# A transformer stack on one core: split operands in four output and two down projections, modulation weights in wide pieces on GpSimd's queue, DeltaNet keys first

## What is computed

```python
def sqrelu_mlp(h, w1, w2):  # 1024 -> 4096 -> 1024, relu squared (mlp0 on 768 columns, mlp1 on 512)
...
h_lat = modulate(rms_norm(x_lat, norm_g[i, 0]), m_lat[:, 0], m_lat[:, 1])
y_ctx, y_lat = mla_mixer(...) or gla_mixer(...)      # end with "@ w_o": mla_out, gla_out
x_lat = x_lat + m_lat[:, 2] * rms_norm(y_lat, norm_g[i, 1])
...
# second block, layer i: mixer 0 is a gated DeltaNet, mixer 1 retention
mod = (e @ ada_w[i] + ada_b[i])[:, None, :]          # 6144 values of modulation
y = mixers[i % N_MIXERS_2](x * (1.0 + sc1) + sh1)    # end with "@ w_out": gdn_out, ret_out
x = layer_norm(DN_ALPHA * x + (1.0 + g1) * y, ln_g[i, 0], ln_b[i, 0])
y = conv_ffn(x * (1.0 + sc2) + sh2, ...)             # up 1024 -> 2 x 2816, down 2816 -> 1024
x = layer_norm(DN_ALPHA * x + (1.0 + g2) * y, ln_g[i, 1], ln_b[i, 1])
```

## Time and profile before

| what | value |
|---|---|
| median of 3 runs | 4176.59 us (4167.09 to 4179.34) |
| profiled run, its own time | 4172.41 us |
| its span, first to last instruction | 4170.6 us |
| TensorE, VectorE, ScalarE busy | 92%, 45%, 27% |
| mean granted TensorE clock | 0.966 |
| mlp0, mlp1 (stretches read) | 692.0 to 1248.2, 1773.4 to 2151.8 |
| DeltaNet pairs | 2213 to 2705 |
| ffn0 up, ffn0 down | 2793.6 to 3028.5, 3028.5 to 3206.4 |
| ffn1 up, ffn1 down | 3746.8 to 3981.7, 3983.7 to 4135.1 |

### The profile page before, as it was taken

One profiled execution on the slowest core, in us unless ns is written; L12 is line 12 of the kernel. 1 busy time (PEld: TensorE's weight loads), 2 busy tenths in 40 slices (PEclk: granted clock), 3 DMA queues, 4 the chain that ended last, 5 costly groups with the idle time before them and its releaser, 6 DMA issues.

```text
span 4170.6 us, 45563 instructions
## 1 busy us (share of the span) xinstructions
PE 3852.7 (92%) x16674; PEld 2768.1 (66%) x16674; DVE 1869.7 (45%) x3568; ACT 1113.7 (27%) x1357; POOL 0.2 (0%) x4
## 2 busy tenths in 40 slices
PE   6899997999998898799989999799998999899998
PEld 3477766999994656377765556548844778548853
DVE  1244426666664333366655445434477443124401
ACT  2111105132224222333333332334301322124301
POOL 0000000000000000000000000000000000000000
PEclk9999999999998999899999999899999999999999
DMA  4121111333330111145531111012376222213231
GB/s 152 41 72 61 66 56 56 102 111 99 101 96 31 31 35 45 44 143 150 152 117 38 41 40 31 28 51 92 104 197 173 66 79 72 71 41 101 92 91 49
DMA packets 414370, 335.19 MB, mean 80 GB/s; under 512 B 11697, under 2 KB 393009, under 8 KB 414129
## 3 DMA queue, kind: packets, MB, share of 16 engines
q1 hardware_dynamic: 408768, 326.21, 25.6%
q10 hardware_dynamic: 5489, 7.47, 0.5%
HBM read 331.55 MB, written 2.10 MB: 80 GB/s over the span
## 4 chain that ended last, share of the span: by engine, by line
PE 83%; DVE 6%; ACT 4%; issue 3%; DMA 2%; ACTq 1%; DVEq 0%; SPq 0%
PE acc L603 62%; PE sc L603 4%; DVE tab L1699 2%; PE sc L1050 2%; PE sc L634 2%; PE acc L798 1%; PE sc L772 1%; PE sc L774 1%; PE sc L637 1%; PE acc L1050 1%; PE acc L1204 1%; DMA wring<-in_mlp_w 1%; DMA tab<-in_ada_w 1%; PE sc L644 1%; ACTq L1308 1%
## 5 line engine op out<-in xcount | busy, mean ns | idle before, releaser
L603 PE MATMUL acc<-arena,wring 128*128 128x512 f32 (+2 forms) x1728 | 707.0, 571 | 39.8 <-DMA wring<-in_ffn_down 9.6
L603 PE MATMUL acc<-x_lo,w_hi 128*128 128x512 f32 (+1 forms) x1728 | 651.8, 377 | 0.0
L603 PEld LDWEIGHTS acc<-arena,wring 128*128 128x128 f32 (+1 forms) x1728 | 320.8, 190 | 386.9 <-issue 307.3
L1358 ACT ACTIVATE w_hi<-wring 128x1024 fp32r<-128x1024 f32 x264 | 264.9, 1051 | 1056.5 <-DMA wring<-in_mlp_w 484.4
L603 PE MATMUL acc<-x_hi_seq,w_hi 128*128 128x512 f32 x1216 | 485.2, 399 | 30.4 <-DVE x_lo L1822 29.8
L1816 DVE TENSOR_TENSOR w_lo<-wring,w_hi 128x1024 fp32r<-128x1024 f32 x264 | 311.5, 1222 | 386.7 <-ACT w_hi L1358 385.5
L603 PE MATMUL acc<-x_hi_seq,w_lo 128*128 128x512 f32 x1216 | 478.4, 393 | 0.0
L603 PEld LDWEIGHTS acc<-x_lo,w_hi 128*128 128x128 f32 x1728 | 329.9, 191 | 47.2 <-issue 1.3
L1699 DVE SCALAR_TENSOR_TENSOR tab<-tab,cs 128x128 f32<-128x128 f32 x960 | 316.4, 351 | 25.8 <-DVE tab L1699 0.2
L603 PEld LDWEIGHTS acc<-x_hi_seq,w_hi 128*128 128x128 f32 x1216 | 231.6, 190 | 92.5 <-issue 31.3
L603 PE MATMUL acc<-hid_hi,w_hi 128*128 128x384 f32 (+1 forms) x768 | 275.1, 358 | 0.0
(11 more groups left out here) (347 smaller groups left out, 4808.8 us busy)
## 6 DMA issues: line engine op xcount, KB each, us to landing
wring<-in_mlp_w SPq DMA_DIRECT2D x64, 1024.0 KB, 5.4
tab<-in_ada_w SPq DMA_DIRECT2D x216, 256.0 KB, 4.8
wring<-in_ffn_up SPq DMA_DIRECT2D x44, 1024.0 KB, 5.0
wring<-in_ada_w SPq DMA_DIRECT2D x12, 2048.0 KB, 7.8
wring<-in_ret_w_in SPq DMA_DIRECT2D x24, 1024.0 KB, 5.2
wring<-in_ffn_down SPq DMA_DIRECT2D x16, 1408.0 KB, 7.1
rstd<-in_ada_w SPq DMA_DIRECT2D x72, 256.0 KB, 5.3
wring<-in_gdn_w_in SPq DMA_DIRECT2D x16, 1024.0 KB, 5.7
```

The costliest lines, as they stand in the source:

```text
L603: ins = pe.matmul(o, lhsT, rhs, start=start, stop=stop)
L1358: f(w_hi[s][:, c], wring[s][:, c], ACT.Copy).then_inc(w_high, 1)
```

## The change

Four edits.

1. The four output projections and both ffn downs become stages of `SPLIT`. Output projections load groups of two units (one in ret_out), ffn downs two groups of 11 blocks a unit, with halves of 704 columns. ScalarE and VectorE make high and low parts of the mixers' outputs (`out_highs`, `out_lows`), and, pair by pair within the ffn up, of the hidden values. The parts lie over memory that is free then (`overlay`); the ups' high inputs lie in two parts of 256 columns (`x_hole`). In mla_out and gla_out the sums of squares of unit j-3 stand ahead of unit j.
2. Modulation pieces are one input block by 512 columns (256 KB, rows of 2 KB), 24 a quarter in three slots, issued by GpSimd on its own queue. Sums come three times a quarter, of 4 column blocks each.
3. ffn0_down's VectorE program puts pieces and weight splits in the order of `DOWN_PIECES`.
4. In `gdn_pair` keys are convolved, squared and normed ahead of queries, both sums of squares (units 1, 2) stand ahead of the row spreads (3, 4), and gate columns 1 (unit 8) behind the products (6, 7).

```diff
-SPLIT = ("mlp0", "mlp1", "ffn0_up", "ret_head", "ffn1_up")
+SPLIT = ("mla_out", "mlp0", "gla_out", "mlp1", "gdn_out", "ffn0_up", "ffn0_down", "ret_head", "ret_out",
+         "ffn1_up", "ffn1_down")
+HALF_COLS = {s: 1024 for s in SPLIT}
+HALF_COLS["ffn0_down"] = HALF_COLS["ffn1_down"] = HIDB * P // 4
...
+MOD_SLOTS = 3
+MOD_N = 512
+MOD_SUM_AFTER = {6: 0, 10: 1, 14: 2}
+DOWN_SUM_AFTER = {(0, 15): 0, (1, 15): 1}
+DOWN_PIECES = ((range(0, 8), range(8, 10), range(10, 14)), (range(14, 22), range(22, 24), range(0)))
...
+        @block.gpsimd
+        def _(pool):
+            for phase, ready in enumerate((16, 32, 40)):
...
+                pool.wait_ge(n_mul, ready)
+                with pool.Fori(0, 4) as it:
+                    for p in range(MOD_PIECES):
+                        i, k = divmod(p, DB)
+                        pool.wait_ge(mod_used[p % MOD_SLOTS], piece(phase, it, p))
+                        pool.dma_start(mod_w[p % MOD_SLOTS], w[:, k, bass.ds(it * (MOD_IT * MOD_N) + i * MOD_N, MOD_N)]
+                                       ).then_inc(mod_loaded[p % MOD_SLOTS], 16)
...
+            def out_proj(stage, nk, per, squares=None):
+                for j in range(8):
+                    if squares and j > 2:
+                        square_sum(*squares, [j - 3])
+                    if j % per == 0:
+                        w = split_group(stage, 0, j // per, nk, per * P)
+                    claim(pe, stage, 0, j)
+                    for k in range(nk):
+                        if j == 0:
+                            pe.wait_ge(o_split, OUT0[stage] + k + 1)
+                        if j % per == 0 and k == nk // 2:
+                            second_half(stage, 0, j // per)
+                        last = split_product(unit(stage, j), w, (j % per) * P, k, out_parts(stage, k), k == 0, k == nk - 1)
+                    last.then_inc(acc_ready, 1)
...
-                for r, (x, y) in enumerate(((d_q, d_Y), (d_k, d_U))):
+                act.wait_ge(d_conv, it * 3 + 2)
+                for j in (1, 0):
+                    act.wait_ge(qk_ready, it * 2 + j + 1)
+                    f(d_cp[:, j, :, 3:SEQ + 3], sc[:, j], ACT.Copy).then_inc(qk_moved, 1)
+                for r, (x, y) in enumerate(((d_k, sq[:, :, 0:SEQ]), (d_q, d_ET))):
                     act.wait_ge(d_conv, it * 3 + r + 3)
                     f(x, x, ACT.Silu).then_inc(d_silu, 1)
                     act.wait_ge(d_silu, it * 3 + r + 1)
+                    f(y, x, ACT.Square).then_inc(d_sq, 1)
+                finished(act, S, it, 0)
+                free(f(d_cp[:, 0, :, 3:SEQ + 3], unit(S, 0), ACT.Copy), S, 0)
+                act.wait_ge(d_done, it * 1 + 1)
+                for j, y in ((1, d_U), (2, d_Y)):
+                    finished(act, S, it, j)
+                    free(f(y, unit(S, j), ACT.Ln, bias=eps[:, 0:1]), S, j)
...
+            act.wait_ge(g_done, GLA_H + 1)
+            high_weights("gla_out", 0, 0)
+            out_highs("gla_out", [g_out[:, b, :] for b in range(DB)])
+            high_weights("gla_out", 0, 1)
...
+                    dve.wait_ge(h2_high, it * 1 + (HIDB // 2 * i + 1))
+                    tt(wide_lo[:, bass.ds(it * 2, 2), :], h, hid2_hi[:, bass.ds(it * 2, 2), :].bitcast(F32), SUB).then_inc(h2_split, 1)
```

More of the change, by code:

```diff
@@ L263, in first_and_second_block @@
         d_vn = carve(2, P)
+        at[0] = D_OUT_AT
         d_out = carve(GDN_H, SEQ)
@@ L377, in x_parts, with hole_parts, out_parts @@
             return [(0, n, x_hi_seq[:, k, :], x_lo[:, k, CTX:T])]
+        def hole_parts(k):
+            return [(0, SEQ, x_hole(k), x_lo[:, k, CTX:T])]
+        def out_parts(stage, k):
+            if stage == "mla_out":
+                return [(h, HALF, x_lo[:, k, t], attn_lo[:, k, t]) for h, t in ((0, slice(0, HALF)), (1, slice(HALF, T)))]
+            if stage == "ret_out":
+                hi = x_lo[:, k, CTX:T] if k < DB else x_hi_seq[:, k - DB, :]
+                return [(0, SEQ, hi, wide_lo[:, k, :])]
+            return [(0, SEQ, x_lo[:, k, CTX:T], {"gla_out": g_out_lo, "gdn_out": d_out_lo}[stage][:, k, :])]
         def finished(eng, stage, it, j):
@@ L688, in mod_sum @@
             def mod_sum(phase, it, i, nv):
[L690 to L693, removed]
-                last.then_inc(mod_summed, 1)
[L696 to L712, removed]
+                p, per = i * DB + DB - 1, MOD_N // P
+                pe.wait_ge(mod_used[p % MOD_SLOTS], piece(phase, it, p) + 1)
+                for m in range(per):
+                    for v in range(nv):
+                        c = MOD_AT + (i * per + m) * nv + v
+                        last = pe.matmul(mod_psum[:, bass.ds(it * (MOD_IT * per * nv) + c, 1)],
+                                         mod_acc[:, i % 2, v, m * P:(m + 1) * P], ones[:, 0:1], start=True, stop=True)
+                last.then_inc(mod_summed, 1)
             w = group("mla_in", 0, 0, DB, Q_RANK)
@@ L806, in _ @@
                     weigh(n)
-            def out_proj(stage, x, n, nk, per):
-                for j in range(8):
-                    if j % per == 0:
-                        w = group(stage, 0, j // per, nk, per * P)
-                    claim(pe, stage, 0, j)
-                    linear(unit(stage, j), w, (j % per) * P, x, n, nk).then_inc(acc_ready, 1)
-            emptied(pe, "mla_pair", 3, 33)
-            out_proj("mla_out", lambda k: attn[:, k, :], T, DB, 4)
             def split_group(stage, it, j, k, n):
@@ L1513, in _ @@
                 f(d_v, d_v, ACT.Silu).then_inc(d_silu, 1)
+                for r, j in ((0, 5), (1, 8)):
+                    finished(act, S, it, j)
+                    free(f(d_z[:, r, :], unit(S, j)[:, 0, :], ACT.Silu), S, j)
                 for l in range(1, 7):
```

463 lines of the change are left out of this document (275 added, 188 removed).

## The result

The changed kernel takes 4133.6 us (4132.2 to 4135.0, 4 runs) where the kernel before took 4174.3 beside it (4167.1 to 4179.3): a ratio of 0.989 (0.988 to 0.991). It is faster, by 41 us, a third of the 125 that the prediction summed, and 4134 lies outside its range of 4010 to 4100.

A forecast was written before the change was run, and what follows sets the result against it. TensorE, busy 92% of the span, was taken as the bound. Savings summed to 125.4 us off the profiled 4172.4, giving 4047, or 4051 with 4.2 to the median, stated as 4050; range 4010 to 4100.

The forecast's parts named there:

- the starts: Output projections: new wait for copies and subtractions before TensorE begins, 4.1 us for gla and gdn, 6.0 mla, 1.4 ret.
- the covers in the down projection: ffn1_down: loading and splitting a group of 11 blocks takes 6.4 us, hidden under TensorE's 7.5 us.
- the terms of gla_out, ret_out and ffn1_down: Net savings from split products in these three stages: 8.7, 22.0 and 32.4 us.
- R: ffn0_down: load time of one 256 KB modulation piece issued by GpSimd, taken as 3.9 us between bounds 2.8 and 5.5.
- The wait for accumulator 0: DeltaNet pair: queries' sum must wait until ScalarE's copy frees this accumulator, at 2358.85, TensorE idle 4.8 us.
- the claim of unit 9: DeltaNet pair: turned keys need unit 7's half, freed only at 2385.5 to 2386.4, against 2387.1 before.
- the term of ffn0_down: Four quarters of eight slot rounds at 4.7 us plus 2 us, 39.6 each: stage 158 us, 20 less.
- 1.5 a pair, 6 in all: DeltaNet keys first: each pair of heads 1.5 us shorter, 6 us less in all.
- it falls in the new gap: DeltaNet pairs, unfavourable end: the clock drops in the new idle gap, making each pair 2 us longer.
- B: Rival, chance 0.11: R stays 5.5 us by sharing DMA engines, ffn0_down 210, MLPs keep their waits, kernel 4121 us.
- D: Rival, chance 0.04: slower than before, R beyond 8 us in ffn0_down; at R of 9 the kernel takes 4214 us.
- C: Rival, chance 0.08: GpSimd's own queue brings nothing in the MLPs, quarter-end waits come from loads themselves; kernel 4069 us.

The follow-up runs named there:

- No_pieces: Changed kernel with ffn0_down's modulation pieces and their sums left out: 0.965 of the kernel before.
- no_sums: Changed kernel with all ffn0_down modulation pieces kept but the 12 sums over them left out: 0.983 of the kernel before.
- order: Changed kernel with ffn0_down's split of the next quarter's second group behind that quarter's first 4 pieces, and sums later: 0.983 of the kernel before.
- slots4: Changed kernel with four places for modulation pieces in ffn0_down instead of three, order unchanged: 0.984 of the kernel before.
- deferred: Changed kernel with ffn0_down reordered, four slots, pieces spread differently and each quarter's third sum made in the next quarter: 4078.3 us, 0.975 of the kernel before.
- half_bytes: The run deferred with each ffn0_down modulation piece loading only half its columns, 128 KB: 0.973 of the kernel before.
- mlp_sync: Changed kernel with both MLPs' modulation pieces issued by SyncE behind weight groups, not by GpSimd: 4127.3 us, 0.987 of the kernel before.
- ups_plain: Changed kernel with both up projections reading the contiguous low input part instead of the high part with holes: 0.988 of the kernel before.

## Why the prediction was wrong

**Right.** The price of a split product (0.681 us at 512 columns, 8.46 a unit at 768), the starts (4.1 us for gla, 1.4 for ret_out), the covers in the down projection, and so the terms of gla_out, ret_out and ffn1_down, each within 1.5 us (for gla_out with some luck, its stretch varies by 3 us). R with no weight load beside it: 3.8 for 3.9. The wait for accumulator 0 and the claim of unit 9 in a pair. Of mla_out's missing 3.1 us, 1.8 lie ahead of the stage.

**The failed step** is in the term of ffn0_down: "eight rounds a quarter, and some 2 us where the order blocks". A quarter took 53.6 us and not 39.6. The order blocked 11.7 us a quarter: 6.9 at the split of the next quarter's group 1 (27.6 in all) and 4.8 at the residual of the first unit (19.2 in all). The rest is rounds longer than the 4.7 us booked, some of them beside weight loads. I counted rounds as if VectorE were free for a piece whenever one landed. Its program is one list, and one entry, the split of the next quarter's group 1, needs a chain that starts only when TensorE has left the quarter: sum, first product, load 4.45, copy 0.80. TensorE in turn left only behind piece 24. A ring closed through four engines, and VectorE took no piece inside it. No_pieces gives the floor, no_sums what leaving out the sums gives (37 us), order and slots4 give the share of the order (28) and of the slots (25), deferred and half_bytes what is left. What would have shown the ring beforehand was at hand: writing one quarter with a time beside each entry of DOWN_PIECES, from rows that I had.

The bounds of R were read wrongly as well. "The highest row of such a piece is 5.5" is not so: these are medians, and the chain of the kernel before has four such pieces of 7.3 to 7.6 us to landing in this very stage, one of them

```profile
3044.79 7.41 DMA tab<-in_ada_w
```

The median of 2.8 there hides them (2.5 to 8.5 us). After the change the pieces took 3.0 to 5.8 us, and beside the weights, with four slots, 4.1 to 4.6 in the median.

**The step that was missing** is the clock behind a wait. A wait was priced at its length. In ffn0_down TensorE's busy time is 154 us for the 139 of deferred, with the same records: some 15 us more, with a mean granted clock of 0.83 for 0.95. The same thing made mlp1's gain 8.4 us larger than its wait, gave every other DeltaNet pair 4.7 us more, and starts gdn_out with products 0.43 us apart.

**DeltaNet.** "1.5 a pair, 6 in all" came out as 3.1 worse in three pairs and 7.8 better in one, net 1.5 worse, which is no more than traces of the same code differ by. The bound of 2 a pair more "(it falls in the new gap)" was the right branch and too small. Of the other 10.6 us of that stretch 4.1 are gdn_out's start, foreseen. The last 6.5 stay open: even with the old pairs back, the first one's lead-in is 3.5 longer than before (80.5 for 77.0), and the end behind the last one some 3.

**Holes.** Nothing was booked for them but a limit (0.72 us a product), which 0.694 kept; they are 9.2 us of the loss.

**Rivals.** B's time, 4121, was the nearest, by its size and not by its cause: the median piece landed in 3.2 us and not in 5.5, and the MLPs lost their waits. D had no part: no piece took more than 5.8 us to land. C was right in its mechanism, that the queue brings nothing, and wrong in what follows, since the waits went anyway. Its counter-evidence, SyncE's 67.4 us, was read wrongly: in mlp_sync SyncE waited 106 us in mlp1, with the ring loaded ahead, and it cost nothing.

## What to carry to other kernels

Where one engine's list serves two streams (pieces that land, weights that another engine lets in), write one period with times and look for an entry that needs the period's own end; rates alone hide it. Price a wait of TensorE by its length and by what runs behind it at the lower clock: here 8 us on 14.5 in one stage. And before giving a stream a queue of its own, ask whether anybody waits for the queue that it leaves.

## What the runs showed of the hardware

- Products of 512 columns whose moving operand lies in two parts of 256 take 0.2292 us (high weights) and 0.2333 us (low weights) apart, the plain one between them 0.2308; with all operands plain each takes 0.227 (ups_plain). In gdn_out plain operands took 0.231 to 0.233 too, in gla_out, with the same form, 0.227: not explained.
- A 256 KB piece from GpSimd took 3.1 to 3.2 us to land in the median with three slots and 165 GB/s moving (the changed kernel), 4.1 to 4.6 with four slots and 224 GB/s (deferred); 128 KB with four slots took 2.6 with 167 GB/s (half_bytes). GpSimd's issue itself takes 0.54 us.
- After gaps of 6 to 10.5 us TensorE's products were 0.43 us apart, with a granted clock of 0.50, for 3 to 7 us in ffn0_down and gdn_out. In the DeltaNet pairs, behind the same waits of 1.8 and 4.4 us, the granted clock stayed at 0.50 for 16 us in one pair; in the next it was back after 4 us and fell again for 3. TensorE was busy all the while in both.
